# Causal masks of two attentions by unit-matrix products, with scores in neighbouring PSUM banks

## The reference, cut to what matters

```python
# second block, one block of 128 queries
s = jnp.einsum('bqhcd,bshcd->bhcqs', q_blk, k) * (d ** -0.5)
causal = kpos[None, :] <= qpos[:, None]
a = jax.nn.softmax(jnp.where(causal, s, -jnp.inf), axis=-1)
diff = a[:, :, 0] - lam * a[:, :, 1]
return jnp.einsum('bhqs,bshe->bqhe', diff, v)

# third block, one block of 128 queries
z = jnp.einsum("bhqd,bhkd->bhqk", q_blk, kf) * scale
mask = k_pos[None, :] < q_pos[:, None]
log_not = jnp.where(mask, jax.nn.log_sigmoid(-z), 0.0)
suffix = lax.cumsum(log_not, axis=3, reverse=True) - log_not
weights = jnp.where(mask, jnp.exp(jax.nn.log_sigmoid(z) + suffix), 0.0)
return jnp.einsum("bhqk,bhkd->bhqd", weights, vf)
```

## Time and profile before

| what | us |
|---|---|
| median of 3 runs | 4244.84 (4240.98 to 4247.27) |
| the profiled execution, its own time | 4255.23 |
| its span | 4253.5 |
| PE busy | 4032.8 (95% of the span) |
| DVE, ACT, POOL busy | 1755.0, 1318.5, 1177.3 |
| rounds of the differential attention | about 2400 to 2575 of the span |
| rounds of the stick-breaking attention | about 3071 to 3265 of the span |

### The profile page before, as it was taken

One profiled execution on the slowest core, in us unless ns is written; L12 is line 12 of the kernel. 1 busy time (PEld: TensorE's weight loads), 2 busy tenths in 40 slices (PEclk: granted clock), 3 DMA queues, 4 the chain that ended last, 5 costly groups with the idle time before them and its releaser, 6 DMA issues.

```text
span 4253.5 us, 59373 instructions
## 1 busy us (share of the span) xinstructions
PE 4032.8 (95%) x26080; PEld 3219.3 (76%) x26080; DVE 1755.0 (41%) x2888; ACT 1318.5 (31%) x2313; POOL 1177.3 (28%) x613
## 2 busy tenths in 40 slices
PE   8899999999999999999999989999988999999998
PEld 4757676766998997676667767697877988888887
DVE  2545454533240248762105572232187332323353
ACT  3232323222232244562113352122275212122133
POOL 1102010112114357661222101243102523333353
PEclk9999999999999999999999999999998999999999
DMA  3101010003011121100111001120100211111111
GB/s 89 32 2 31 2 31 2 16 16 111 31 41 50 40 80 40 35 21 30 35 45 50 30 1 43 47 92 20 50 1 21 70 50 50 50 50 41 49 50 40
DMA packets 164978, 168.68 MB, mean 40 GB/s; under 512 B 8176, under 2 KB 152432, under 8 KB 164720
## 3 DMA queue, kind: packets, MB, share of 16 engines
q1 hardware_dynamic: 164720, 164.89, 12.2%
HBM read 156.48 MB, written 8.39 MB: 39 GB/s over the span
## 4 chain that ended last, share of the span: by engine, by line
PE 78%; DVE 12%; ACT 4%; POOL 3%; issue 3%; DMA 0%; POOLq 0%; SPq 0%; DVEq 0%; ACTq 0%
PE bank L627 15%; PE bank L629 15%; PE bank L628 15%; PE bank L592 9%; PE bank L615 3%; PE bank L1104 3%; PE bank L603 2%; PE bank L1119 1%; PE bank L582 1%; PE bank L777 1%; PE bank L1270 1%; POOL H L3422 1%; PE bank L769 1%; PE bank L1294 1%; PE bank L895 1%
## 5 line engine op out<-in xcount | busy, mean ns | idle before, releaser
L627 PE MATMUL bank<-XT_r,W_r 128*128 128x512 f32 x1744 | 700.8, 402 | 8.4 <-ACT BIG L1969 1.9
L628 PE MATMUL bank<-BIG_r,W_r 128*128 128x512 f32 x1624 | 632.5, 389 | 0.0
L3364 POOL TENSOR_TENSOR W_r<-W,W_r 128x2048 fp32r<-128x2048 f32 (+1 forms) x74 | 309.2, 4179 | 760.4 <-ACT W_r L1432 760.4
L629 PE MATMUL bank<-XT_r,W_r 128*128 128x512 f32 x1232 | 481.1, 390 | 0.0
L627 PE MATMUL bank<-W_r,BIG_r 128*128 128x256 f32 (+1 forms) x1280 | 418.0, 327 | 1.4 <-DVE MIX_r L2705 0.4
L592 PE MATMUL bank<-XT,W 128*128 128x512 f32 x928 | 405.5, 596 | 3.2 <-POOL MIX L3237 2.2
L627 PEld LDWEIGHTS bank<-XT_r,W_r 128*128 128x128 f32 x1744 | 328.2, 188 | 88.6 <-issue 14.2
L629 PE MATMUL bank<-W_r,BIG_r 128*128 128x256 f32 (+1 forms) x1152 | 380.4, 330 | 0.0
L628 PEld LDWEIGHTS bank<-BIG_r,W_r 128*128 128x128 f32 x1624 | 305.3, 188 | 71.9 <-issue 10.3
L592 PEld LDWEIGHTS bank<-XT,W 128*128 128x128 f32 x928 | 175.1, 191 | 220.1 <-issue 218.6
L629 PE MATMUL bank<-W_r,MIX_r 128*128 128x256 f32 x960 | 272.1, 283 | 0.0
(11 more groups left out here) (427 smaller groups left out, 7803.6 us busy)
## 6 DMA issues: line engine op xcount, KB each, us to landing
W<-w_in SPq DMA_DIRECT2D x29, 1024.0 KB, 5.5
W<-w_in_e SPq DMA_DIRECT2D x33, 512.0 KB, 6.4
MIX<-w_up SPq DMA_DIRECT2D x15, 1024.0 KB, 5.3
MIX<-w_down SPq DMA_DIRECT2D x15, 1024.0 KB, 4.9
W<-w_in_o SPq DMA_DIRECT2D x12, 1024.0 KB, 5.1
W<-w_in SPq DMA_DIRECT2D x17, 512.0 KB, 4.1
H<-x SPq DMA_DIRECT2D x16, 512.0 KB, 9.5
W<-w_out SPq DMA_DIRECT2D x7, 1024.0 KB, 5.1
```

The costliest lines, as they stand in the source:

```text
L627: E.matmul(b[:, 0:n], lh, rh, start=k == ks[0], stop=False)
L628: E.matmul(b[:, 0:n], lh, rl, start=False, stop=False)
L629: mm = E.matmul(b[:, 0:n], ll, rh, start=False, stop=k == ks[-1])
L3364: G.tensor_tensor(WLO[k % 2][:, 0:n], WSTAGE[k % 2][:, 0:n], WHI[k % 2][:, 0:n], ALU.subtract).then_inc(*s_split.mark("split", k))
```

## The change

The mask is no longer added by DVE. After the scores of a row block PE multiplies the unit matrix `ident` by the mask (`MC` or `MN`, 128x128) into the last 128 columns of the last bank, without clearing it, so that it adds up there; the last score product no longer ends its group and its semaphore moves to that mask product. The eight banks are now declared as four pairs of neighbours (2 x 512 columns). The banks of one map (or head) are opened one after the other, so that a score row of up to 1024 columns lies in one pair, and `wide` gives it as one operand: one maximum on DVE, one exponential with one sum on ACT, and two sigmoids on ACT, where two banks took twice as many. With i above 3 the waits for free banks change in the differential attention: PE now waits for all four ahead of the first score product, where it waited for each bank ahead of its own product. The combining of two maxima and of two sums is gone.

```diff
+        pairs = [ctx.enter_context(nc.psum_tensor(f"pair{i}", [P, 2 * HALF], F32)) for i in range(4)]
+        banks = [pairs[i // 2][:, i % 2 * HALF:(i % 2 + 1) * HALF] for i in range(8)]
+    def wide(self, *name, n):
+        at = self.place.get(name, 0) % len(self.banks)
+        return self.pairs[at // 2][:, at % 2 * HALF:at % 2 * HALF + n]
...
                 for _, i, h in diff_items(r, 0):
                     n = (i + 1) * P
+                    for c in range(2):
+                        for k0 in range(0, n, HALF):
+                            for_diff.open("diff", "s", i, h, c, k0)
+                            pe.wait_ge(*for_diff.free("diff", "s", i, h, c, k0))
                     for k0 in range(0, n, HALF):
                         kn = min(HALF, n - k0)
                         for c in range(2):
                             pr = slice(64 * c, 64 * c + 64)
-                            b = for_diff.open("diff", "s", i, h, c, k0)
-                            pe.wait_ge(*for_diff.free("diff", "s", i, h, c, k0))
-                            E.matmul(b[:, 0:kn], QT_D[pr, h, i * P:(i + 1) * P], KT_D[pr, h, k0:k0 + kn], start=True,
-                                     stop=True).then_inc(*diff.pe.mark("diff", "s", i, h, c, k0))
+                            b = for_diff.bank("diff", "s", i, h, c, k0)
+                            mm = E.matmul(b[:, 0:kn], QT_D[pr, h, i * P:(i + 1) * P], KT_D[pr, h, k0:k0 + kn], start=True,
+                                          stop=k0 + kn < n)
+                            if k0 + kn < n:
+                                mm.then_inc(*diff.pe.mark("diff", "s", i, h, c, k0))
+                    pe.wait_ge(*done("diff", "mask"))
+                    for c in range(2):
+                        E.matmul(for_diff.bank("diff", "s", i, h, c, k0)[:, kn - P:kn], ident[:, :], MC, start=False,
+                                 stop=True).then_inc(*diff.pe.mark("diff", "s", i, h, c, k0))
...
+            pe.wait_ge(*done("stick", "consts"))
+            for h in (2 * ct, 2 * ct + 1):
+                E.matmul(for_stick.bank("stick", "s", i, h, k0)[:, kn - P:kn], ident[:, :], MN, start=False,
+                         stop=True).then_inc(*stick.pe.mark("stick", "s", i, h, k0))
...
-                        for j, k0 in enumerate(range(0, n, HALF)):
-                            kn = min(HALF, n - k0)
-                            S.activation(dst[:, k0:k0 + kn], for_diff.bank("diff", "s", i, h, c, k0)[:, 0:kn], ACT.Exp,
-                                         bias=st_d(k)[:, c:c + 1], accum_out=st_d(k)[:, 4 + 2 * j + c:5 + 2 * j + c]).then_inc(
-                                             *diff.act.mark("ev", "diff", "s", i, h, c, k0))
+                        S.activation(dst[:, 0:n], for_diff.wide("diff", "s", i, h, c, 0, n=n), ACT.Exp,
+                                     bias=st_d(k)[:, c:c + 1], accum_out=st_d(k)[:, 4 + c:5 + c]).then_inc(
+                                         *diff.act.mark("ev", "diff", "s", i, h, c, 0))
...
-                    act.wait_ge(*done("stick", "masked", i, h))
...
-                    for k0 in range(0, n, HALF):
...
-                        S.activation(B_S[k % 2][:, k0:k0 + kn], b[:, 0:kn], ACT.Sigmoid, scale=-1.0).then_inc(
-                            *stick.act.mark())
-                        S.activation(A_S[k % 3][:, k0:k0 + kn], b[:, 0:kn], ACT.Sigmoid).then_inc(
-                            *stick.act.mark("ev", "stick", "s", i, h, k0))
+                    act.wait_ge(*done("stick", "s", i, h, i // 4 * HALF))
+                    b = for_stick.wide("stick", "s", i, h, 0, n=n)
+                    S.activation(B_S[k % 2][:, 0:n], b, ACT.Sigmoid, scale=-1.0).then_inc(*stick.act.mark())
+                    S.activation(A_S[k % 3][:, 0:n], b, ACT.Sigmoid).then_inc(
+                        *stick.act.mark("ev", "stick", "s", i, h, 0))
...
             for c in range(2):
-                b = for_diff.bank("diff", "s", i, h, c, k_last)
...
-                V.tensor_tensor(b[:, kn - P:kn], b[:, kn - P:kn], MC, ALU.add).then_inc(*diff.dve.mark())
...
+                dve.wait_ge(*done("diff", "s", i, h, c, i // 4 * HALF))
+                V.tensor_reduce(st_d(k)[:, c:c + 1], for_diff.wide("diff", "s", i, h, c, 0, n=n), AX.X, ALU.max,
+                                negate=True).then_inc(*diff.dve.mark("diff", "max", k, c))
...
-                for _, i, h in stick_items(r, 0):
...
-                    V.tensor_tensor(b[:, kn - P:kn], b[:, kn - P:kn], MN, ALU.add).then_inc(
-                        *stick.dve.mark("stick", "masked", i, h))
```

More of the change, by code:

```diff
@@ L62, with __init__ @@
 class Banks:
-    def __init__(self, banks, done):
-        self.banks, self.done, self.order, self.place = banks, done, [], {}
+    def __init__(self, banks, pairs, done):
+        self.banks, self.pairs, self.done, self.order, self.place = banks, pairs, done, [], {}
     def open(self, *name):
@@ L204, in build @@
         MIXL = MIX_R[:, :].rearrange("p (c n) -> p c n", c=KD)
-        banks = [ctx.enter_context(nc.psum_tensor(f"bank{i}", [P, HALF], F32)) for i in range(8)]
+        pairs = [ctx.enter_context(nc.psum_tensor(f"pair{i}", [P, 2 * HALF], F32)) for i in range(4)]
+        banks = [pairs[i // 2][:, i % 2 * HALF:(i % 2 + 1) * HALF] for i in range(8)]
         WS = [WS0, WS1]
@@ L299, in ring @@
         def ring(first, n):
-            rings.append(Banks(banks[first:first + n], done))
+            rings.append(Banks(banks[first:first + n], pairs[first // 2:(first + n + 1) // 2], done))
             return rings[-1]
@@ L1260, in pe_scores @@
             n = (i + 1) * P
-            for k0 in range(0, n, HALF):
-                for h in (2 * ct, 2 * ct + 1):
+            for h in (2 * ct, 2 * ct + 1):
+                for k0 in range(0, n, HALF):
                     for_stick.open("stick", "s", i, h, k0)
@@ L2106, in act_stick_rounds @@
                         act.wait_ge(*done("stick", "a_read", k - 3))
[L2107 to L2114 removed]
+                    act.wait_ge(*done("stick", "s", i, h, i // 4 * HALF))
[3 more added lines that the diff above has]
+                        *stick.act.mark("ev", "stick", "s", i, h, 0))
+                    if n > HALF:
+                        stick.act.note("ev", "stick", "s", i, h, HALF)
                     stick.act.note("stick", "sigmoids", k)
@@ L2940, in dve_diff @@
             dve.wait_ge(*done("diff", "neg_lam"))
-            dve.wait_ge(*done("diff", "mask"))
             keep = 1.0 - LAM_INIT
@@ L3005, in dve_diff_weights @@
             dve.wait_ge(*done("diff", "exp", k))
-            if n > HALF:
-                V.tensor_tensor(s[:, 4:6], s[:, 4:6], s[:, 6:8], ALU.add).then_inc(*diff.dve.mark())
-                dve.wait_ge(*diff.dve.last())
             V.reciprocal(s[:, 8:10], s[:, 4:6]).then_inc(*diff.dve.mark())
```

34 lines of the change are left out of this document (7 added, 27 removed).

## The result

The changed kernel took 4214.15 us, the median of 4 runs (4212.46 to 4226.18), beside 4242.91 for the kernel before, the median of 4 (4239.30 to 4247.27). The ratio is 0.9936, 95% interval 0.9920 to 0.9952: 27 us less by the ratio, 29 by the medians. The forecast was 4231, range 4221 to 4255. The direction was right and the size was not: the gain is twice what was forecast, and outside the range.

What follows compares the result with a forecast made beforehand. Bound: PE and DVE both full in differential block 6, a ring of waits in stick-breaking block 7, DVE then PE in later blocks. Terms of -0.6 and -13.1 gave -13.7, so 4241.5 profiled and a median of 4231; range 4221 to 4255.

Steps and rivals of the forecast that it cites:

- Block 6, +2.4: Differential attention, block 6: four rounds of 5.4 us each against 4.80 before, 2.4 us slower.
- closed ring: Differential attention, blocks 7 to 4: an item's scores wait for both exponentials before; rounds of 6.0, 5.4, 4.9, 4.2 us.
- Block 7, +3.5: Differential attention, block 7, at the lower clock: rounds of 8.2 us against 6.60 and 7.64, about 3.5 us slower over three.
- The clock in this attention, -3: Differential attention: shorter PE gaps take something under half off four short clock falls of about 1.8 us; -3 (0 to -7).
- Blocks 5 and 4, -0.7: Differential attention: two PE-bound dummy rounds pay +1.0 for masks, earlier maxima save 1.7; together 0.7 us less.
- Blocks 3 to 0, -2.8: Differential attention: eight rounds led by DVE save 0.35 us each, eight with dummies hide the saving; -2.8 (0 to -10).
- Stick-breaking, -13.1: Whole stick-breaking attention: -1.4 and -1.5 in blocks 7 to 4, -3.2 in 3 and 2, -7 in 1 and 0.
- the likeliest case: Stick-breaking attention, blocks 1 and 0: the clock holds at the higher rate; 4231 us in all (4222 to 4238), chance 0.42.
- The rival of a slower kernel: Differential attention, blocks 7 to 4: PE's 0.4 us gap every round lets the clock drop; 4255 to 4267 us, chance 0.17.
- Dear masks: Both attentions: a mask product takes 0.4 us on the path, some +10, 4241; chance 0.15 shared with dear wide reads.
- A wide read at the price of two narrow ones, +5: Rings of both banks' reads: each gains 0.5 us in 16 items, +5; chance 0.15 shared with dearer masks.
- line between the 1.49 and the 1.80: Stick-breaking attention: PE gaps of 1.49 us leave the clock alone, 1.80 does not; gaps of 1.1 to 1.3 should hold.

Runs made afterwards that it cites:

- masks_only: Kernel before with masks as PE products in both attentions, every operation and wait still on one bank; 4226.42 us, ratio 0.9953 to the kernel before.
- wide_only: Changed kernel with the masks added by DVE again, wide operations kept; 4240.05 us, ratio 0.9987 to the kernel before.
- before_bare: Kernel before without any dummy product in the differential attention; 4229.65 us against 4243.54, ratio 0.9966.
- diff_only: Kernel before with the change in the differential attention alone, the other attention as before; 4234.95 us against 4245.66, ratio 0.9980.
- mixed: Changed kernel with blocks 7 and 6 of the differential attention as before (loop order, waits, masks, narrow operations); 4215.86 us, ratio 0.9937 to the kernel before.
- lean_o: Changed kernel without the 20 dummy products ahead of the output transposes of blocks 7 and 6 of the differential attention; 4214.61 us, ratio 0.9931 to the kernel before.
- masks_both: Kernel before with mask products added on PE in both attentions while DVE still adds its masks; 4245.14 us against 4242.28, ratio 1.0004.

## Why the prediction was right, and where it was wrong

Forecast and measurement, term by term (measured: after minus before in the table, where one pair of traces serves):

- **Block 6, +2.4: measured +2.4.** The closed ring was read rightly in kind (chain of waits above). The rounds took 5.6, 5.6, 5.6 and 5.3, where before had 5.0, 4.9, 5.0 and 4.8: both somewhat longer than the forecast's 5.4 and 4.80, the ring by its second mask.
- **Block 7, +3.5: measured +0.5.** The forecast took 6.60 us for the first of before's rounds, from a row of scores that began at 2413.65. That row is not whole, it has six of the eight records. Timeline of PE in before, with all of them:

```profile
2411.93 5.50 PE L1156 MATMUL bank<-H 64*128 64x512 f32 x8 [4.31 <-ACT BIG L2023]
```

  So the round took 8.32, no shorter than the forecast's ring of 8.2. The later rounds took 8.8, 7.8 and 5.9 after, and 8.3, 6.8 and 5.1 before: +2.3 together. The first one went from 9.6 to 7.8. Timeline of all engines in the second trace of before:

```profile
2397.30 4.49 POOL L3364 TENSOR_TENSOR W_r<-W,W_r 128x2048 fp32r<-128x2048 f32 x1 [19.86 <-ACT W_r L1432]
2397.78 4.02 DVE L2996 TENSOR_TENSOR STAT<-STAT 128x1 f32<-128x1 f32 x1
...
2401.84 0.69 ACT L2023 ACTIVATE BIG<-bank,STAT 128x512 f32<-128x512 f32 x1 [4.62 <-DVE STAT L2996]
```

And in after:

```profile
2391.20 4.50 POOL L3355 TENSOR_TENSOR W_r<-W,W_r 128x2048 fp32r<-128x2048 f32 x1 [19.35 <-ACT W_r L1452]
...
2393.50 2.35 DVE L3000 TENSOR_REDUCE STAT<-pair 128x1 f32<-128x1024 f32 x2 [5.42 <-PE pair L1170]
```

  The combination of two maxima, 0.16 us elsewhere, took 4.02 beside POOL's sum of 4.49 and held ACT for 4.62; two wide maxima ran beside the same POOL sum in 2.35, no longer than their 1.22 each. I had put the 14.2 us of the earlier trace rows mostly just ahead of the dummies of blocks 5 and 4.
- **The clock in this attention, -3: measured about -8. This is the step that failed most.** The forecast counted four short falls and took something under half of them off. All four went, two in blocks 5 and 4 and two in blocks 3 to 0, at 1.5 to 1.6 us each (34 dummy records in 5.69 and 4.06, 24 in 4.57 and 2.94), and so did a fifth just behind the last scores, for which there was no term (dummies in 3.17 instead of 4.76). The forecast's own widest case was -7.
- **Blocks 5 and 4, -0.7: measured -5.0, of it about -3.2 the clock and -1.8 the rest.** Here too a step failed. It said that in the two dummy rounds PE is the bound, so that masks cost 1.0 there and earlier maxima save 1.7. PE was not the bound ahead of the dummies: it idled 2.47 and 2.42 us there, and these waits shrank by 1.47 and 1.43. The round of block 5 fell from 16.4 to 13.8, its fellow in block 4 from 12.5 to 10.2.
- **Blocks 3 to 0, -2.8: measured -4.1, of it -3.2 the clock and -0.9 the rest.** With the forecast's -3 for the clock the sum, -5.8, comes near what these blocks and the dummies behind them lost (-6.1), but that is luck: the saving by DVE was too large there and the clock's too small. masks_only has all of the -4.1, wide_only nothing of it.
- **Nothing counted behind the attention.** The stretch between was 499.1 to 500.6 in six kernels with after's form of the masks and dummies there, and 502.7 to 504.6 in five with DVE's masks. 2.0 of it are the dummies just named with the wait ahead of them; the rest is one or two falls of the clock of 1.6 us each, hundreds of us later in code that no edit touches. That they go with the change I can only report: before_bare, without any change, had 499.3. Behind the last item of the other attention 1.8 us more are gone (991.3 to 989.5), and why was not looked into.
- **Stick-breaking, -13.1: measured -15 (186.3 to 171.1).** Right in the sum, not in its parts: blocks 7 to 4 gave -8 (119.2 to 111.0; forecast -2.9), blocks 3 and 2 -1 to -3 (forecast -3.2), blocks 1 and 0 -4 (22.0 to 18.3; forecast -7). Pairs of block 7 went from 8.2 to 7.9 (forecast 8.0). diff_only, which had no fall of the clock in blocks 6 and 5, took 114.7 for blocks 7 to 4: so about half of the -8 is falls that no longer come, and the other half is shorter rounds. In blocks 1 and 0 the trace that the forecast was read from had the longest fall of all; against it they gave -7.7. The clock held there in all kernels with masks on PE alone, as the likeliest case had it.
- **The rival of a slower kernel** (the closed ring lets the clock drop in blocks 7 to 4) did not come. PE idled 0.54 to 0.89 us in each round of block 6 at a clock of 1.00. By the Trainium skill's page "TensorE: Matmul & The Clock Gate", section "A second HAM failure mode: psum-queue depth-cycling", such small idles can make the clock oscillate; the trace of after does not show it in this ring.
- **Dear masks** (0.4 on the path): 0.14 to 0.18 was measured. The Trainium skill's "TensorEngine Tiling (Array Packing)", Key Properties, says that a change of the tiling mode drains the engine. No price of it shows here at the switch from 64 to 128 rows: two masks behind the scores take 0.43 in the chain above, less than twice 0.25.
- **A wide read at the price of two narrow ones, +5:** it did not come (1.220 against 1.38), and the sum was wrong too: 0.5 in each of 16 items is 8.

At bottom the forecast valued a DVE mask by the engine's busy share of a stretch, on the path in blocks 3 and 2 and half hidden elsewhere, and gave the clock small terms of its own. Measured, a mask taken off DVE is worth 0.28 us of 0.29 on the mean if nothing replaces it and 0.15 to 0.17 if a product does, and very unevenly: next to nothing in blocks 7 and 6 of the differential attention, over 0.3 in the stick-breaking one, with the clock in it. The whole change is then some 20 us for the masks moved from DVE to PE and 7 to 12 more for the wide operations on top (masks_only to after), 27 to 29 in all.

## What to carry to other kernels

- Where several engines pass small pieces round a ring, an engine's busy share of the page says little on what its operations are worth. DVE was busy for 41% of the span, and leaving out 37 us of its work gave 36. Nor is there one price for each operation: the same product cost the path nothing while DVE masked too, and 0.14 to 0.18 us when it didn't. Test both orders of a two-part change before adding prices up.
- See that a row of a timeline is whole (x8, not x6) before a period is read from its start.
- Before a term is priced at "this round has filler work, so PE is the bound", look at the idle time ahead of the filler and at the clock under it. Then try without the filler: it had become a loss of 13 us, unrelated to the change.
- When executions differ by more than the effect, compare stretches that repeat to 0.1 us, as the rounds here do, and take only the end from the medians. mixed and lean_o show that what a stretch gains need not show at the end.

## What the runs showed of the hardware

The length of one gap of PE doesn't tell whether the clock falls behind it. In after the clock stayed at 1.00 around this gap of 1.84 us. In block 3 of the other attention it fell to 0.50 some 2 us behind this one of 1.43, with another gap of 0.96 between (timeline of PE):

```profile
2476.96 1.35 PE L1164 MATMUL pair<-H 64*128 64x512 f32 x8 [1.84 <-ACT BIG L2041]
...
3175.49 1.10 PE L1314 MATMUL pair<-BIG,XT 128*128 128x64 f32 x8 [1.43 <-ACT XT L1442]
```

The forecast had drawn a line between the 1.49 and the 1.80 of the earlier trace rows; these rows do not bear it out. In the code between the attentions, the same gap of 1.88 us, ahead of the same eight transposes, had a fall behind it in before and none in after (17.90 us to the next such place, and 16.28).

More work on PE raised the granted clock without shortening anything: 0.88 and 0.89 over the two attentions in before, 0.93 and 0.96 in masks_both, with a ratio of 1.0004 from end to end.

A tiny operation of DVE on 128x1 elements lasted 4.02 us (4.01 in the other trace of before) while POOL summed 128x2048 elements, and two large reductions of DVE from PSUM beside the same POOL operation were not slowed (2.35 us for two of 1.22). Which of DVE's operands makes the difference was not tried.
